# Rows of the experts gathered by a table of tokens, in place of rows scattered to their slots

## The chip, the cores and the metric

The kernel runs on one core of a Trainium2 chip. That core has TensorE (PE), VectorE (DVE), ScalarE (ACT), GpSimd (POOL) and SyncE (SP), and 16 DMA engines that all queues share. The metric is the time of one execution on the device, in microseconds, the median of several runs.

## What is computed

One step of a two-layer network over 640 tokens (128 context, 512 latent) of 1024 numbers. Layer 0 mixes tokens by attention, layer 1 by retention; each is followed by a mixture of 16 experts in 4 groups. The part that matters here, shortened:

```python
scores = sigmoid(x @ router_w)
grouped = (scores + router_b).reshape(n, 4, 4)
group_score = sum(top_k(grouped, 2)[0], axis=-1)       # the two best of each group
best = argmax(group_score)                             # one group per token
_, idx = top_k(where(group == best, grouped, -inf), 2) # two experts of that group
wts = take(scores, idx) / sum
# blocks of 128 slots, each of one expert; every (token, expert) pair gets a slot
xb = x[tok]                                            # rows of a block
hid = silu(xb @ w_gate[e]) * (xb @ w_up[e])
yb = (hid @ w_down[e]) * wt
y = zeros_like(x).at[row_tok].add(yb)
```

640 tokens with 2 experts each make 1280 pairs. Slots that hold no pair may compute anything, since nothing reads their result with a weight.

## The kernel before, in words

The program is a sequence of stages. Each stage is a block in which every engine has its own list of instructions, ordered by semaphores; all engines pass the end of a stage together. The stages are: setup, modulation, the attention's projection (`mla_project`) and its head pairs, then routing, experts and combine of layer 0, then retention, routing, experts and combine of layer 1, and the output.

**Routing** (`route`, L1430 to L1627). SP issues six weight loads of 2 MB for the first two expert blocks. The normed activations lie with features on the partitions. PE makes the router's logits, then turns all activations into token rows (L1585), which ScalarE copies to the tile `rows` (L1613). VectorE runs one long chain in which each instruction waits for the one before (`link`): the scores, the sum of the two best of each group as the maximum over the six pair sums (L1498 to L1502), the best group, the two best experts as one-hots, the weights, and after PE's prefix sums the row number of both slots of each token (`dest`, L1549). Each expert owns one block of 128 slots, and pairs past 128 go to further blocks, whose expert is worked out at the tail of the chain (L1552 to L1562), together with the number of block pairs to run. POOL waits for `dest` and writes the rows to the DRAM tensor `rows_in` by ten indirect DMAs (L1625): five token tiles, two slots each. It waits for all ten.

**Experts** (`experts`, L1641 to L1952). A loop over blocks of 128 slots, two per turn, as many turns as the routing found (18 blocks in each layer here). Per block POOL loads 128 consecutive rows of `rows_in` (L1695), PE turns them (L1746), ScalarE and VectorE split rows and weights into a high and a low part (L1826, L1895), and PE makes three products for each (L1758). SP refills a weight slot when its last part has been split (L1638). ScalarE stores each result block to `rows_out` (L1851). A refill of rows waits until PE has turned the block two before it (L1699).

**Combine** (`combine`, L1955). POOL gathers both result rows of each token with ten indirect DMAs (L1968) by `dest`.

Because slots without a token are read too, `mla_project` writes zeros over all of `rows_in` (26 stores, L491) and over ten blocks of `rows_out` (L493), from SP.

## Time and profile before

| | us |
|---|---|
| median of 3 runs | 2322.36 (2321.2 to 2327.05) |
| the profiled execution | 2347.12 |
| its span, first to last instruction | 2345.4 |
| PE busy | 2061.8 (88%) |
| VectorE busy | 1155.7 (49%) |
| ScalarE busy | 894.8 (38%) |
| POOL busy | 119.6 (5%) |

The span is what the rows below are timed in. Busy time counts an engine's instructions only, not its waits; the times of PE are modelled at their ends. An entry of a timeline gives start, duration, engine, line, output and inputs, count, and in brackets how long the engine had been idle and what released it.

### The profile page before, as it was taken

What the parts mean: (1) busy time and instruction counts of PE and PEld (TensorE: products, weight loads), DVE (VectorE), ACT (ScalarE), POOL (GpSimd) and SP (SyncE); (2) the same over time, 40 slices, a digit from 0 to 9 for tenths busy, and PEclk for the clock granted to TensorE, in tenths of its full rate; (3) what the DMA queues carried; (4) which work ended last, traced back from release to release, by engine and by line L of the source; (5) the groups of instructions that cost most, each with busy time, mean ns of one, the idle gap of its engine ahead of it and who ended that gap; (6) DMA issues with size and microseconds to landing.
All of it is one profiled execution on the core that took longest, in us unless ns stands there. A gap on an engine that the chain in (4) does not pass through costs nothing. (4 is left out here: it accounts for less than half of the span.)

```text
span 2345.4 us, 25093 instructions
## 1 busy us (share of the span) xinstructions
PE 2061.8 (88%) x8790; PEld 1428.8 (61%) x8790; DVE 1155.7 (49%) x1688; ACT 894.8 (38%) x1251; POOL 119.6 (5%) x139
## 2 busy tenths in 40 slices
PE   4878999999749999958999999999999948999984
PEld 2334545544438878837756865875676427878863
DVE  1122223222559999955322422322242347999975
ACT  1011212212238888824211221221122127888853
POOL 0000000000020000011000100100010010000001
PEclk8679889887869999968999999999999968999995
DMA  9995000100569999734211220221110078999933
GB/s 356 387 379 215 19 28 9 37 18 0 215 234 385 399 399 399 296 139 155 81 45 55 72 90 18 72 81 63 45 63 18 2 303 295 399 399 398 398 151 135
DMA packets 181343, 425.26 MB, mean 181 GB/s; under 512 B 10622, under 2 KB 22427, under 8 KB 181275
## 3 DMA queue, kind: packets, MB, share of 16 engines
q1 hardware_dynamic: 164912, 365.52, 42.3%
q0 software_dynamic: 10944, 39.85, 4.5%
q10 hardware_dynamic: 5418, 18.96, 2.0%
q8 instruction: 45, 0.74, 0.1%
q14 instruction: 24, 0.19, 0.0%
HBM read 369.09 MB, written 55.21 MB: 181 GB/s over the span
## 5 line engine op out<-in xcount | busy, mean ns | idle before, releaser
L1895 DVE TENSOR_TENSOR moe_w_lo<-weight_ring,moe_w_hi 128x1024 fp32r<-128x1024 f32 x432 | 520.3, 1222 | 84.4 <-ACT moe_w_hi L1826 70.2
L1826 ACT ACTIVATE moe_w_hi<-weight_ring 128x1024 fp32r<-128x1024 f32 x432 | 456.5, 1061 | 192.7 <-PE ps L1758 124.5
L1758 PE MATMUL ps<-moe_w_hi,moe_rows_t_hi 128*128 128x512 f32 x576 | 232.8, 404 | 5.1 <-DVE moe_rows_t_lo L1900 4.7
L1305 DVE TENSOR_TENSOR ret_w_lo<-weight_ring,ret_w_hi 128x512 fp32r<-128x512 f32 x128 | 95.4, 746 | 274.5 <-ACT ret_w_hi L1227 274.5
L1758 PE MATMUL ps<-moe_w_hi,moe_rows_t_lo 128*128 128x512 f32 x576 | 226.5, 393 | 0.0
L1758 PE MATMUL ps<-moe_w_lo,moe_rows_t_hi 128*128 128x512 f32 x576 | 226.0, 392 | 0.0
L1100 PE MATMUL ps<-ret_w_hi,h_hi 128*128 128x512 f32 x480 | 193.9, 404 | 3.6 <-ACT weight_ring L1231 2.5
L1227 ACT ACTIVATE ret_w_hi<-weight_ring 128x512 fp32r<-128x512 f32 x128 | 80.8, 635 | 302.8 <-PE ps L1100 299.9
L1100 PE MATMUL ps<-ret_w_lo,h_hi 128*128 128x512 f32 x480 | 189.6, 395 | 0.0
L1100 PE MATMUL ps<-ret_w_hi,h_lo 128*128 128x512 f32 x480 | 189.5, 395 | 0.0
L1758 PEld LDWEIGHTS ps<-moe_w_hi,moe_rows_t_hi 128*128 128x128 f32 x576 | 109.5, 190 | 27.1 <-DVE moe_rows_t_lo L1900 5.5
L1758 PEld LDWEIGHTS ps<-moe_w_hi,moe_rows_t_lo 128*128 128x128 f32 x576 | 109.1, 189 | 23.7
L1758 PEld LDWEIGHTS ps<-moe_w_lo,moe_rows_t_hi 128*128 128x128 f32 x576 | 109.6, 190 | 20.8
L1758 PE MATMUL ps<-moe_w_hi,moe_hidden_t_hi 128*128 128x512 f32 x288 | 114.6, 398 | 3.0 <-DVE moe_hidden_t_lo L1905 3.0
L1758 PE MATMUL ps<-moe_w_lo,moe_hidden_t_hi 128*128 128x512 f32 x288 | 113.8, 395 | 0.0
L1758 PE MATMUL ps<-moe_w_hi,moe_hidden_t_lo 128*128 128x512 f32 x288 | 113.7, 395 | 0.0
L1212 PE MATMUL ps<-weight_ring 128*128 128x512 f32 x256 | 110.9, 594 | 2.9 <-ACT weight_ring L1292 2.9
L1100 PEld LDWEIGHTS ps<-ret_w_hi,h_hi 128*128 128x128 f32 x480 | 90.0, 187 | 29.3 <-issue 5.3
L1100 PEld LDWEIGHTS ps<-ret_w_lo,h_hi 128*128 128x128 f32 x480 | 90.0, 188 | 23.0 <-issue 1.9
L1100 PEld LDWEIGHTS ps<-ret_w_hi,h_lo 128*128 128x128 f32 x480 | 90.0, 187 | 22.0
L1187 PE MATMUL ps<-weight_ring 128*128 128x512 f32 x224 | 99.7, 593 | 2.2 <-DVE weight_ring L1316 2.2
L307 PE MATMUL ps<-weight_ring,silu_cond 128*32 128x512 f32 x384 | 67.5, 841 | 33.4 <-DMA weight_ring<-in_ada_w 20.6
(303 smaller groups left out, 2979.9 us busy)
## 6 DMA issues: line engine op xcount, KB each, us to landing
weight_ring<-in_moe_w_gate SPq DMA_DIRECT2D x36, 2048.0 KB, 13.7
weight_ring<-in_moe_w_up SPq DMA_DIRECT2D x36, 2048.0 KB, 14.7
weight_ring<-in_moe_w_down SPq DMA_DIRECT2D x36, 2048.0 KB, 14.1
weight_ring<-in_ada_w SPq DMA_DIRECT2D x24, 2048.0 KB, 19.8
weight_ring<-in_ret_w_in SPq DMA_DIRECT2D x12, 2048.0 KB, 9.1
h_normed<-rows_in POOLq DMA_DIRECT2D x36, 512.0 KB, 7.1
rows_out<-h_normed ACTq DMA_DIRECT2D x36, 512.0 KB, 6.3
rows_in<-zero_rows SPq DMA_DIRECT2D x26, 512.0 KB, 15.1
```

Source lines behind the costliest of these rows:

```text
L307: mm = pe.matmul(ps[32 * j:32 * j + 32, n % 4, :], cond[:, k, :], weights(n)[:, k, :], start=(half == 0), stop=(half == 1), tile_position= ...
L1100: mm = pe.matmul(out, lhs, rhs, start=(k == 0 and x == 0), stop=(k == KD - 1 and x == 2))
L1187: mm = pe.matmul(out, lhs, rhs, start=(x == 0), stop=(x == len(mms) - 1))
L1212: mm = pe.matmul(ps[:, bank(f"w{d}"), :], wo[:, b, d * P:(d + 1) * P], yt[:, b, SEQ:T], start=(b == 0), stop=(b == 3))
L1227: nc.scalar.activation(whi[:, n % BUF, :], win[s][:, k, :], ACT.Identity).then_inc(w_hi, 1)
L1305: dve.tensor_tensor(wlo[:, n % BUF, :], win[s][:, k, :], whi[:, n % BUF, :].bitcast(F32), ALU.subtract).then_inc(w_lo, 1)
L1758: mm = pe.matmul(out, lhs, rhs, start=(first and x == 0), stop=(last and x == 2))
L1826: nc.scalar.activation(whi[:, x, :], part(u, w + x), ACT.Identity).then_inc(w_hi, 1)
L1895: dve.tensor_tensor(wlo[:, x, :], part(blk[1], w + x), whi[:, x, :].bitcast(F32), ALU.subtract).then_inc(w_lo, 1)
```

## The change

In routing ScalarE stores the token rows plainly to the first 640 rows of `rows_in` (five stores). VectorE makes, beside `dest`, for each slot index k and token tile a one-hot of the slot's place in its block (128 wide) and a one-hot of its block (26 wide) multiplied by the token's number. PE multiplies the two and sums over tokens, which gives a table of 128 places by 26 blocks that holds the token of each slot, and 0 where a slot has none. VectorE copies it to `tok` as integers. POOL's scatters are gone. In the expert loop POOL copies the block's column of the table and gathers the 128 rows by it. The 26 stores of zeros to `rows_in` are gone; those to `rows_out` stay. The sum of a group's two best is made from maxima and minima of pairs: 7 instructions in place of 11. Two constants (a row 0 to 127 and the token numbers) come by a small load at the start of routing. Semaphores of the combine live through both layers, and five small tiles of retention become parts of one.

```diff
-            one * np.arange(NBLK), p % 32 == np.arange(NE)]
+            one * np.arange(NBLK), p % 32 == np.arange(NE), one * np.arange(P), p + P * np.arange(NT)]
...
-        self.xs = ops["rows_in"]
+        self.xs = ops["rows_in"][0:T, :]
...
-                for b in range(NBLK):
-                    sp.dma_start(c.xs[b * P:(b + 1) * P, :], zeros[:, :]).then_inc(zeros_out, 16)
...
+                sp.dma_start(consts[:, :], c.ops["base_consts"][:, _width(BASE_COLS):]).then_inc(const_in, 16)
                 prefetch(sp)
...
+                link(dve.tensor_scalar(by_row[:, :], c.base["iotab"], float(P), None, ALU.mult))
...
-                m = gr[:, :, :].rearrange("p t (g e) -> p (t g) e", e=EG)
-                link(dve.tensor_tensor(pair[:, 0, :], m[:, :, 0], m[:, :, 1], ALU.add))
-                for a in range(EG):
-                    for b in range(max(a + 1, 2), EG):
-                        link(dve.tensor_tensor(pair[:, 1, :], m[:, :, a], m[:, :, b], ALU.add))
-                        link(dve.tensor_tensor(pair[:, 0, :], pair[:, 0, :], pair[:, 1, :], ALU.max))
-                first_best(keep[:, :, :], pair[:, 0, :].rearrange("p (t g) -> p t g", t=NT), NG)
+                grouped = gr[:, :, :].rearrange("p t (g e) -> p (t g) e", e=EG)
+                two = gr[:, :, :].rearrange("p t (h e) -> p (t h) e", e=2)
+                more, less = top2[:, 0, :], top2[:, 1, :]
+                link(dve.tensor_tensor(more, two[:, :, 0], two[:, :, 1], ALU.max))
+                link(dve.tensor_tensor(less, two[:, :, 0], two[:, :, 1], ALU.min))
+                more, less = (x.rearrange("p (g h) -> p g h", h=2) for x in (more, less))
+                first, second, third = top2[:, 2, 0:G], top2[:, 2, G:2 * G], top2[:, 3, 0:G]
+                link(dve.tensor_tensor(first, more[:, :, 0], more[:, :, 1], ALU.max))
+                link(dve.tensor_tensor(second, more[:, :, 0], more[:, :, 1], ALU.min))
+                link(dve.tensor_tensor(third, less[:, :, 0], less[:, :, 1], ALU.max))
+                link(dve.tensor_tensor(second, second, third, ALU.max))
+                link(dve.tensor_tensor(first, first, second, ALU.add))
+                first_best(keep[:, :, :], first.rearrange("p (t g) -> p t g", t=NT), NG)
...
-                mark["dest"] = n
+                link(dve.tensor_scalar(slot_i[:, :, :], c.dest[:, :, :], P - 1, None, ALU.bitwise_and))
+                link(dve.tensor_copy(slot[:, :, :], slot_i[:, :, :]))
+                link(dve.tensor_tensor(blk[:, :, :], dst[:, :, :], slot[:, :, :], ALU.subtract))
+                dve.wait_ge(const_in, 16)
+                for k in range(2):
+                    link(dve.tensor_tensor(at_slot[:, k], m["iota"].unsqueeze(1).to_broadcast([P, NT, P]),
+                                           slot[:, k, :].unsqueeze(2).to_broadcast([P, NT, P]), ALU.is_equal))
+                    for t in range(NT):
+                        link(dve.tensor_scalar(at_blk[:, k, t, :], by_row[:, :], blk[:, k, t:t + 1], m["token"][:, t:t + 1],
+                                               ALU.is_equal, ALU.mult))
+                    mark[f"at{k}"] = n
...
+                dve.wait_ge(mapped, 1)
+                dve.tensor_copy(c.tok[:, :], ps[:, 7, 0:NBLK])
...
+                    pe.wait_ge(chain, mark[f"at{k}"])
+                    for t in range(NT):
+                        mm = pe.matmul(ps[:, 7, 0:NBLK], at_slot[:, k, t, :], at_blk[:, k, t, :],
+                                       start=(k == 0 and t == 0), stop=(k == 1 and t == NT - 1))
+                mm.then_inc(mapped, 1)
...
+                    if g % 2:
+                        act.wait_ge(taken, g + 1)
+                        act.dma_start(c.xs[(g // 2) * P:(g // 2 + 1) * P, :], rows[:, g // 2, :]).then_inc(stored, 16)
+                act.wait_ge(stored, 16 * NT)
...
-                pool.wait_ge(chain, mark["dest"])
-                for t in range(NT):
-                    pool.wait_ge(taken, 2 * t + 2)
-                    for k in range(TOPK):
-                        pool.indirect_dma_start(c.xs, bass.IndirectOffsetOnAxis(c.dest[:, k, t:t + 1], 0),
-                                                rows[:, t, :], None).then_inc(scattered, 16)
-                pool.wait_ge(scattered, 16 * NT * TOPK)
...
                 def load_rows(blk):
-                    b, u, _ = blk
-                    pool.dma_start(xr[:, u, :], c.xs.rearrange("(b p) d -> b p d", p=P)[bass.ds(b, 1)].rearrange("a p d -> (a p) d"))\
-                        .then_inc(xfull[u], 16)
+
+                    b, u, i = blk
+                    pool.tensor_copy(tok[:, u:u + 1], c.tok[:, bass.ds(b, 1)]).then_inc(indexed, 1)
+                    pool.wait_ge(indexed, b + 1)
+                    pool.sem_inc(c.asked, 1)
+                    pool.indirect_dma_start(xr[:, u, :], None, c.xs, bass.IndirectOffsetOnAxis(tok[:, u:u + 1], 0)).then_inc(xfull[u], 16)
 
                 def refill_rows(blk):
                     pool.wait_ge(turned, blk[0] - 1)
+                    pool.sem_inc(c.asked, 1)
                     load_rows(blk)
```

## Rows read from the trace of the kernel before

**Rows 1.** The page, part 1: busy us (share of the span) and instructions.

```profile
PE 2061.8 (88%) x8790; PEld 1428.8 (61%) x8790; DVE 1155.7 (49%) x1688; ACT 894.8 (38%) x1251; POOL 119.6 (5%) x139
```

**Rows 2.** Waits, 670 to 1010 us: who, for whom, total, times, longest.

```profile
ACT moe_w_hi L1826 <- PE ps L1758: 62.1, 171, 4.3
```

**Rows 3.** Windows: length, busy by engine, clock, DMA share, GB/s; loop, combine.

```profile
700.00:940.00 240.00, 236.18 (x1107) 192.60 (x1106) 225.76 (x211) 196.37 (x212) 6.99 (x13) 1.00 1.04 395
...
1026.00:1036.00 10.00, 3.83 (x16) 3.13 (x16) 4.49 (x10) 3.44 (x3) 7.06 (x7) 0.50 0.97 359
```

**Rows 4.** Timeline, 600 to 720 us: routing of layer 0.

```profile
609.17 1.01 DVE L898 SCALAR_TENSOR_TENSOR x_resid<-ps,modulation,x_resid 128x128 f32<-128x128 f32 x2 [1.15 <-PE ps L799]
...
610.53 0.31 POOL L1617 MEMSET route_router<- 128x256 f32 x1 [449.29 <-POOLq L681]
...
632.80 4.56 PE L1585 MATMUL ps<-base_consts,h_normed 128*128 128x128 f32 x40
...
633.33 0.20 DVE L1493 TENSOR_SCALAR route_scores<-route_scores 128x80 f32<-128x80 f32 x1 [1.70 <-ACT route_scores L1609]
...
634.53 0.20 DVE L1498 TENSOR_TENSOR route_pair<-route_biased 128x20 f32<-128x20 f32 x1
...
636.78 0.18 DVE L1502 TENSOR_TENSOR route_pair<-route_pair 128x20 f32<-128x20 f32 x1
...
644.29 2.29 PE L1597 MATMUL ps<-route_both,base_consts 128*128 128x16 f32 x10
...
652.18 0.17 DVE L1549 CAST route_rows<-route_dst 128x10 int32<-128x10 f32 x1
...
654.28 0.53 DVE L1562 TENSOR_SCALAR block_pairs<-route_turns 128x1 int32<-128x1 f32 x3
...
664.22 0.95 POOL L1625 DMA_INDIRECT rows_in<-route_rows  x1 [0.31 <-issue]
670.00 1.15 POOL L1695 DMA_DIRECT2D h_normed<-rows_in  x2 [4.82 <-POOLq L1453]
...
671.74 4.63 DVE L1895 TENSOR_TENSOR moe_w_lo<-weight_ring,moe_w_hi 128x1024 fp32r<-128x1024 f32 x4 [16.93 <-ACT moe_w_hi L1826]
...
673.68 1.97 PE L1746 MATMUL ps<-base_consts,h_normed 128*128 128x128 f32 x8 [27.09 <-DMA h_normed<-rows_in]
```

**Rows 5.** Timeline, 1870 to 2000 us: routing of layer 1.

```profile
1917.81 0.17 DVE L1549 CAST route_rows<-route_dst 128x10 int32<-128x10 f32 x1
...
1939.12 1.97 PE L1746 MATMUL ps<-base_consts,h_normed 128*128 128x128 f32 x8 [26.90 <-DMA h_normed<-rows_in]
```

**Rows 6.** Single lines of VectorE: duration in ns, least, median, most.

```profile
L424 DVE TENSOR_TENSOR h_normed<-x_resid,norm_rstd x32: 818/820/826, 164.4 to 2332.5; 128x640 f32<-128x640 f32 x32
...
L430 DVE TENSOR_SCALAR h_normed<-h_normed,norm_amplitude,modulation x16: 341/344/348, 165.8 to 1893.8; 128x128 f32<-128x128 f32 x16
```

**Rows 7.** DMA issues, KB, median us to landing: 700 to 940, then 900 to 960.

```profile
rows_out<-h_normed ACTq DMA_DIRECT2D x13, 512.0 KB, 6.3
...
weight_ring<-in_moe_w_gate SPq DMA_DIRECT2D x3, 2048.0 KB, 15.2
```

**Rows 8.** Lines 1695 (loads of rows) and 1968 (combine's gathers): issues, landing.

```profile
L1695 POOL DMA_DIRECT2D h_normed<-rows_in x36: 527/537/584, 670.0 to 2209.4; - x36
...
DMA to landing us min/median/max: 3.5/7.1/7.8
...
DMA to landing us min/median/max: 4.3/5.6/6.2
```

**Rows 9.** Timeline of SP and POOL in the expert loop of layer 0.

```profile
677.12 0.38 SPq L1638 DMA_DIRECT2D weight_ring<-in_moe_w_gate  x1
...
743.12 0.54 POOL L1695 DMA_DIRECT2D h_normed<-rows_in  x1 [17.73 <-PE ps L1746]
```

**Rows 10.** Zero stores in the attention's projection (timeline), and a wait of SP.

```profile
154.09 27.10 SPq L491 DMA_DIRECT2D rows_in<-zero_rows  x26
...
SPq L495 <- DVE mla_new_cache L599: 38.2, 1, 38.2
```

More of the change, by code:

```diff
@@ L73 @@
 BASE_COLS = {"ident": P, "ones": P, "before": P, "iota16": NE, "iota4": NG, "iotab": NBLK, "pick": NE}
+ROUTE_COLS = {"iota": P, "token": NT}
 MLA_COLS = {"swap": P, "rcos": LAT, "rsin": LAT}
@@ L148, in __init__ @@
         self.w_in_full, self.wq_full, self.wkv_full, self.wo_full = sems(nc, stack, "mla", ["w_in", "wq_full", "wkv_full", "wo_full"])
+        self.comb_sems = sems(nc, stack, "comb", ["weighed", "summed", "turned", "added"])
+        self.got = sems(nc, stack, "comb", [f"got{t}" for t in range(NT)])
+        self.asked, = sems(nc, stack, "moe", ["rows_asked"])
         self.ret_full = sems(nc, stack, "ret", [f"full{s}" for s in range(4)])
-        self.xs = ops["rows_in"]
+        self.xs = ops["rows_in"][0:T, :]
         self.ys = ops["rows_out"]
@@ L1022, in retention @@
         qd = sb("q_decayed", [P, 2, LAT])
-        kd, lg = sb("k_decay", [P, 2]), sb("log_decay", [P, 2])
-        sumsq, mean, rs = sb("sumsq", [P, NT, 2]), sb("meansq", [P, NT, 2]), sb("rstd", [P, NT, 2])
+        small = sb("small", [P, 4 + 6 * NT])
+        kd, lg = small[:, 0:2], small[:, 2:4]
+        sumsq, mean, rs = (small[:, 4 + 2 * NT * x:4 + 2 * NT * (x + 1)].rearrange("p (t f) -> p t f", f=2) for x in range(3))
         half = c.half[:, 0:2]
@@ L1442, in route @@
                                              ("scores", "biased", "masked", "one1", "one2", "both", "tmp", "past"))
-        pair, keep, off = sb("pair", [P, 2, G]), sb("keep", [P, NT, NG]), sb("off", [P, NT, NG])
+        consts = sb("consts", [P, _width(ROUTE_COLS)])
+        m = _views(consts, ROUTE_COLS)
+        slot_i = sb("slot_int", [P, 2, NT], I32)
+        slot, blk = sb("slot", [P, 2, NT]), sb("block", [P, 2, NT])
+        at_slot, at_blk = sb("at_slot", [P, 2, NT, P]), sb("at_block", [P, 2, NT, NBLK])
+        top2, keep, off = sb("pair", [P, 4, 2 * G]), sb("keep", [P, NT, NG]), sb("off", [P, NT, NG])
         top = sb("top", [P, NT])
@@ L1448, in route @@
         cmp, eb, tn = sb("compare", [P, NBLK - NE, NE]), sb("block_e", [P, NBLK]), sb("turns", [P, 2])
+        by_row = sb("block_rows", [P, NBLK])
         logits_t = sb("logits_t", [P, T])
         norm = Norm(c, st, 2 * layer + 1, amp, shift)
-        padded, by_expert, copied_a, copied_v, logits, ranks, turned, taken, expd, chain, scattered = sems(
-            nc, st, f"route{layer}", ["padded", "by_expert", "copied_a", "copied_v", "logits", "ranks", "turned", "taken", "exp", "chain", "scattered"])
+        padded, by_expert, copied_a, copied_v, logits, ranks, turned, taken, expd, chain, const_in, stored, mapped = sems(
+            nc, st, f"route{layer}", ["padded", "by_expert", "copied_a", "copied_v", "logits", "ranks", "turned", "taken", "exp", "chain", "consts", "stored", "mapped"])
         with nc.Block(no_gpsimd_drain=True) as block:
@@ L1598, in _ @@
                 mm.then_inc(ranks, 1)
+                for k in range(2):
+                    pe.wait_ge(chain, mark[f"at{k}"])
[3 more added lines that the diff above has]
+                mm.then_inc(mapped, 1)
             @block.scalar
@@ L1662, in experts @@
         sil, hid = sb("silu", [P, FE]), sb("hidden", [P, FE])
+        tok = sb("tokens", [P, 2], I32)
+        indexed, = sems(nc, st, f"moe{layer}", ["indexed"])
         xfull = sems(nc, st, f"moe{layer}", ["x_full0", "x_full1"])
@@ L1960, in combine @@
         y = st.enter_context(nc.sbuf_tensor(f"comb{layer}_rows", [P, NT, TOPK, D], F32))
-        got = sems(nc, st, f"comb{layer}", [f"got{t}" for t in range(NT)])
-        weighed, summed, turned, added = sems(nc, st, f"comb{layer}", ["weighed", "summed", "turned", "added"])
+        got = c.got
+        weighed, summed, turned, added = c.comb_sems
+        before = layer * NT
         with nc.Block(no_gpsimd_drain=True) as block:
@@ L1979, in _ @@
                 for t in range(NT):
-                    pe.wait_ge(summed, t + 1)
+                    pe.wait_ge(summed, before + t + 1)
                     if t >= 4:
-                        pe.wait_ge(added, (t - 3) * KD)
+                        pe.wait_ge(added, (before + t - 3) * KD)
                     for k in range(KD):
@@ L1991, in _ @@
                     if t < NT:
-                        dve.wait_ge(weighed, t + 1)
+                        dve.wait_ge(weighed, before + t + 1)
                         dve.scalar_tensor_tensor(out=y[:, t, 0, :], in0=y[:, t, 1, :], scalar=c.w12[:, 1, t:t + 1],
@@ L1996, in _ @@
                         n = t - 1
-                        dve.wait_ge(turned, n + 1)
+                        dve.wait_ge(turned, before + n + 1)
                         jc = 0 if n == 0 else 1
```

9 lines of the change are left out of this document (5 added, 4 removed).

## The prediction, made before the result was known

> **What bounds the kernel now.** I read the page first, then the waits of an expert stage, then the stretches of it by window, then the routing stage instruction by instruction. On the page [rows 1] TensorE is busy 88% of the span. Two expert stages (from about 670 us and from about 1936 us) take 36 block turns [rows 8]. The waits of the first [rows 2] say which is late there: ScalarE's weight splits wait for PE 171 times (62.1 us in all), and no weight split waits for a DMA. The loop's stretch [rows 3] shows PE busy 236.18 of 240 us at full clock, and DMA share 1.04 at 395 GB/s: PE sets the pace, DMA is just short of setting it. So the expert loop is expensive, but what the change shortens lies before it, where PE is idle 27.1 us [rows 4].
>
> In the first layer's routing [rows 4] VectorE runs one dependent chain of small instructions, one start every 0.21 to 0.28 us, and finishes the slot numbers at 652.35. POOL then issues ten scatters, 1.26 us apart, 652.67 to 665.17. It waits for them to land, all engines pass the stage's end, and POOL issues the first load of rows at 669.97. The rows land and PE starts to turn them at 673.68. From the end of the slot numbers to the first turned row: 673.68 - 652.35 = 21.33 us. In the second layer [rows 5] it is 1939.12 - 1917.98 = 21.14 us. Nothing else is late in that time: the first four weight splits end at 676.4 on VectorE [rows 4], and the turned rows, which take 2 us on PE and then both engines in turn, come after them.
>
> **The change part by part, per layer.**
>
> Two best of a group. Before, 11 instructions, 634.53 to 636.99, 2.46 us [rows 4]. After, 7: two over 40 elements (between the 0.18 us of 20 and the 0.24 of 80; I take 0.21), three over 20 strided at 0.20, two over 20 plain at 0.18, each with 0.03 to the next: 0.48 + 0.69 + 0.42 = 1.6 us. Saved 0.86 us. The added product for the block rows stands ahead of a wait in which VectorE idles 1.70 us: free.
>
> Longer chain on VectorE after the slot numbers:
> - three instructions on 10 elements at about 0.17 + 0.03 each: 0.62 us;
> - two comparisons of 128x640. The row is the norm's product of that size, 0.82 us [rows 6]; with the gap 0.85, so 1.70 us;
> - ten instructions on 26 elements with two scalars read from SBUF. No row is that form: at 128 elements it takes 0.344 us [rows 6], a plain one on 20 elements 0.18 us [rows 4]. Taking off 102 elements at the 0.24 - 0.18 us per 60 of the chain's rows gives 0.24; with the gap 0.26, so 2.6 us. Ends: 2.1 to 3.7 us.
> Then the old tail, from 652.35 to 654.81 (its last three start at 654.28), 2.46 us [rows 4]. PE's last five products of 26 columns start beside that tail. Their nearest row is the count of the experts, ten records in 2.29 us [rows 4]: with the handover, hidden to within 0.1 us. The copy of the table adds 0.2. From slot numbers to VectorE's end: 0.62 + 1.70 + 2.6 + 2.5 + 0.2 = 7.62 us (7.1 to 9.0).
>
> Ten scatters removed. With them go their 12.5 us of issue, the landing of the last, and 10 x 512 KB of writes. What is late next is VectorE's end above.
>
> Five stores from ScalarE. They are issued from about 634.5 to 641, while the six weight loads still run. Those are 12.6 MB from 611 us and end near 643 at the loop's 395 GB/s [rows 3]. Adding 2.6 MB puts everything down by about 650. In the expert loop, where DMA is as full, a 512 KB store lands in 6.3 us [rows 7]. VectorE ends at 652.35 - 0.86 + 7.62 = 659.1, so 9 us of cover. The weights pushed back by 6.7 us are first needed after 659. Were the cover gone, each us past it would cost one. The ScalarE issues stretch the copies by some 2 us and PE's turning by as much; PE's turning now ends at 637.4 and PE is next wanted some 4.8 us later, five instructions before its count at 644.29 [rows 4], so that is covered too. SP issues one 68 KB load ahead of its six: 0.4 us, hidden for the same reason.
>
> Start of the experts. The last stage change of this kind took 0.35 us from VectorE's last instruction (610.18) to POOL's first (610.53) [rows 4]. POOL then copies one column (no row; its fill of 256 elements takes 0.31 us [rows 4], so I take 0.25 with the wait, ends 0.1 and 0.6) and issues a gather in place of a plain load. The plain load landed 3.5 us after its issue at best, the combine's gathers 4.3 at best, 5.6 in the median when ten queue up [rows 8]. The first stands alone, so 4.3, with ends 3.5 and 6.2.
>
> Sum, from slot numbers to the first turned row: -0.86 + 7.62 + 0.35 + 0.25 + 4.3 = 11.66 us. Saved: 21.33 - 11.66 = 9.67 and 21.14 - 11.66 = 9.48; together **19.2 us**. Ends: 11 to 22 us. The loop starts that much earlier whichever engine bounds it, since DMA too stands still before its first refill at 677.12 [rows 9].
>
> The Trainium skill gives a different price for that first gather: "DMA: Bandwidth & Descriptors", section on the anatomy of a SWDGE DMA, fits 2.0 us plus the bytes at 436 GB/s, which is an estimate of 3.2 us for 512 KB. The rows show 3.5 for the plain load and 4.3 for a gather, so the trace disagrees and I keep 4.3; by the skill's fit the sum would be 21.4 us.
>
> Gathers inside the loop. POOL refills a row buffer as soon as it is turned, and idles 17.7 us between refills [rows 9]; a dearer issue (0.95 of a scatter [rows 4] against 0.54 us), a copy and a wait vanish in that. Bytes and packets are the same 512 KB.
>
> Zero rows. The 26 stores of zeros are issued 154.1 to 181.2, ten more behind them; SP then waits 38.2 us for VectorE's last row of the stage [rows 10]. Nothing of value is freed: 0 us. Renamed semaphores, the constants' split and the shared small tile change no instruction on the path: 0.
>
> The profiled execution took 2347.12 us (span 2345.4), the median of the timed ones 2322.36, 1.1% less. 2347.12 - 19.2 = 2327.9; for the median 2322.36 - 19.2 x 0.989 = **2303.4 us**.
>
> **Rivals.**
>
> A, slower: the row that all empty slots read. 18 blocks have 2304 slots, 1280 hold a token, and the other 1024 now read token 0, 57 slots a block, 0.233 MB from one 4 KB row. Before, each slot had its own row. DMA has no room: three 2 MB loads, a load of rows and a store are 7.34 MB, and a block turn takes 17.73 + 0.54 = 18.27 us [rows 9]: 402 GB/s. A weight slot is used every second block, 36.5 us; its four parts are split in a third of a turn, 6 us, so about 30 us are left from refill to next use, and the load takes 15.2 us late in the stage [rows 7], some with 2 us more: 13 us of slack. If those 57 reads cost e more per block, the loop loses 18e - 13 us per layer. It decides from e = 0.72 us, and eats the gain at e = (13 + 9.6)/18 = 1.26 us, which is the row served at 0.233 MB/(0.58 + 1.26 us) = 127 GB/s. At a quarter of full rate (100 GB/s, e = 1.75) each layer loses 18.5 and gains 9.6: +17.8 us, 2340 us. For it: nothing in this trace reads one row many times, and DMA is full. Against it: the combine's gathers of scattered rows run at 359 GB/s [rows 3], no worse than plain traffic.
> The Trainium skill has a rule of this sort ("DMA: Bandwidth & Descriptors", section on latency and other measured facts): streams in step on aliased HBM rows fell from 207 to 103 GB/s. No run here shows it; halved, e is 0.6 us and hides in the slack.
>
> B, smaller gain: the chain and the first gather come out at their dear ends (9.0, 6.2, copy 0.6, some wait for PE), 5.5 to 6 us saved per layer: 2311 us. For it: several forms have no row, and the first gather already reads the shared row. Against it: the chain's other rows are very regular.
>
> C, no change: the scatters were not what held the stage, because the stores of ScalarE land late, queued behind 12.6 MB of weights. They would have to land at 669, 18 us after the sum of bytes allows. Gain 0, 2322 us. Against it: the 6.3 us landing in the full loop.
>
> **How the numbers follow.** Forecast 0.74, A 0.07 (slower) and 0.02 (its loss near the gain, no change), B 0.14, C 0.03. The likeliest own range is 2299 to 2309. The 8 in 10 range takes B in: 2298 to 2311. A measurement here tells about 0.3% (7 us) from no change: faster 0.74 + 0.14 = 0.88, same 0.02 + 0.03 = 0.05, slower 0.07.
>
> **What would show it.** Ten instructions of the 26-element form per layer at about 0.24 us; VectorE's part of the routing ending 6.8 us after where its slot numbers ended; POOL starting the experts some 10.5 us earlier against the routing's start; a first gather landing in about 4.3 us; the block period still 18.2 to 18.3 us with no weight split waiting for a DMA. Wrong it would be if that period grows, if weight loads take over 25 us, or if the routing stage ends on ScalarE's stores.

## The result

On the chips on which both kernels ran, the kernel before had a median of 2332.4 us over 22 runs (2316.0 to 2352.1) and the changed one 2319.0 us over 22 (2301.5 to 2334.1). The ratio is 0.9939, 95% interval [0.9915, 0.9964]: 14.2 us less (8.4 to 19.8). Run again, the changed kernel gave 2320.6 us over 12 runs against 2331.5 over 14: 0.9957 [0.992, 0.9994]. Three more runs of the kernel before, at 2350.8 to 2352.8 us, fell into a slower state of the chip and are left out there. The forecast was 2303.4 us, from 2298 to 2311. So it named the right side and missed the size: the gain is smaller than the 19.0 us forecast, and the kernel before, too, is 10 us slower over 22 runs than over the three that were known.

The profiled execution of the changed kernel took 2334.08 us (span 2331.9, granted clock 0.915), 13.0 us less than that of the kernel before. Its page, part 1 (busy time, share and instructions by engine), answers to [rows 1]:

```profile
span 2331.9 us, 25267 instructions
...
PE 2070.7 (89%) x8830; PEld 1438.1 (62%) x8830; DVE 1164.7 (50%) x1714; ACT 895.8 (38%) x1251; POOL 141.3 (6%) x155
```

POOL is busy 22 us longer, for its gathers are dearer to issue than plain loads. It waits for most of each turn, so this costs nothing in the loop. The loop itself, as in [rows 3] (length, busy time by engine, clock, DMA share, GB/s):

```profile
691.00:931.00 240.00, 236.17 (x1106) 192.54 (x1106) 225.71 (x211) 196.41 (x212) 24.41 (x26) 1.00 1.04 395
```

PE is busy 236.17 of 240 us, before 236.18, at the same DMA share. Thirteen blocks, from the start of turning block 2 to that of block 15, took 237.05 us, before 236.99.

The routing of layer 0 in the changed kernel, as in [rows 4] (start, duration, engine, line, operation, count, idle time before it and what ended it):

```profile
609.42 0.31 POOL L1660 MEMSET route_router<- 128x256 f32 x1 [449.11 <-POOLq L684]
...
633.43 0.20 DVE L1515 TENSOR_TENSOR route_pair<-route_biased 128x40 f32<-128x40 f32 x1
...
634.75 0.18 DVE L1523 TENSOR_TENSOR route_pair<-route_pair 128x20 f32<-128x20 f32 x1
634.97 0.17 DVE L1497 TENSOR_REDUCE route_top<-route_pair 128x5 f32<-128x20 f32 x1
...
639.72 0.33 ACTq L1655 DMA_DIRECT2D rows_in<-route_rows  x1
...
650.06 0.17 DVE L1570 CAST route_rows<-route_dst 128x10 int32<-128x10 f32 x1
650.27 0.17 DVE L1571 TENSOR_SCALAR route_slot_int<-route_rows 128x10 int32<-128x10 int32 x1
...
650.89 0.82 DVE L1576 TENSOR_TENSOR route_at_slot<-route_consts,route_slot 128x640 f32<-128x640 f32 x1
651.75 1.64 DVE L1579 TENSOR_SCALAR route_at_block<-route_block_rows,route_block,route_consts 128x26 f32<-128x26 f32 x5
...
654.29 1.64 DVE L1579 TENSOR_SCALAR route_at_block<-route_block_rows,route_block,route_consts 128x26 f32<-128x26 f32 x5
655.96 0.33 DVE L1583 TENSOR_TENSOR route_compare<-route_cumulated,base_consts 128x160 f32<-128x160 f32 x1
655.98 2.33 PE L1635 MATMUL ps<-route_at_block,route_at_slot 128*128 128x26 f32 x10 [0.20 <-DVE route_at_block L1579]
...
658.42 0.18 DVE L1595 CAST block_tokens<-ps 128x26 int32<-128x26 f32 x1 [0.17 <-PE ps L1635]
658.96 0.18 POOL L1734 COPY moe_tokens<-block_tokens 128x1 int32<-128x1 int32 x1 [41.67 <-POOLq L1466]
660.04 1.17 POOL L1737 DMA_INDIRECT h_normed<-rows_in,moe_tokens  x1 [0.90 <-POOL moe_tokens L1734]
...
664.47 1.97 PE L1788 MATMUL ps<-base_consts,h_normed 128*128 128x128 f32 x8 [6.16 <-DMA h_normed<-rows_in,moe_tokens]
```

The reader sees the whole path of the change here: slot numbers done at 650.23, VectorE done at 658.60, first gather issued at 660.04, PE starts to turn the first rows at 664.47. That is 8.37 + 1.44 + 4.43 = 14.24 us, where it was 21.33. In layer 1 it is 13.92, where it was 21.14. From start to slot numbers the stage took 40.81 and 41.57 us, before 41.82 and 43.12.

The table gives these parts for every kernel profiled, in us (the experiments that the names stand for follow below): from routing's start to the slot numbers; from there to VectorE's end, to the gather's issue and to the first turned row, with their sum; then from the issue of the last store of the experts to the first gather of the combine. A dash stands where a kernel has no such part.

```
kernel, layer     start-slots  VectorE  to issue  to row    sum   store-combine
before       0       41.82        -        -       3.68    21.33      3.85
before       1       43.12        -        -       3.61    21.14      3.81
changed      0       40.81       8.37     1.44     4.43    14.24      5.97
changed      1       41.57       8.36     1.35     4.21    13.92      3.75
again        0       40.77       8.36     1.44     4.44    14.24      5.98
again        1       39.67       8.35     1.35     4.27    13.97      3.76
two_best     0       41.53        -        -       3.72    21.36      3.84
two_best     1       41.73        -        -       3.65    21.20      3.81
zeros_kept   0       41.50       8.35     1.43     4.48    14.26      5.97
zeros_kept   1       41.42       8.35     1.35     4.24    13.94      3.74
pad24        0       39.63       8.35     1.44     4.51    14.30      3.76
pad24        1       41.56       8.37     1.35     4.26    13.98      3.74
pad64        0       39.64       8.37     1.44     4.43    14.24      3.77
pad64        1       41.59       8.37     1.69     4.23    14.28      3.75
no_copy      0       41.49       8.36     1.09     4.56    14.01      3.78
no_copy      1       41.75       8.37     0.99     4.23    13.59      3.77
wide_blocks  0       39.63       7.08     1.44     4.65    13.17      6.13
wide_blocks  1       39.92       7.08     1.35     4.24    12.67      3.76
own_rows     0       41.52       8.42     1.43     4.06    13.92      6.49
own_rows     1       41.66       8.42     1.34     3.99    13.76      3.74
one_row      0       41.52       8.36     1.43     4.55    14.34      6.18
one_row      1       41.52       8.36     1.34     4.47    14.17      3.75
warm         0       41.47       8.36     1.44     5.42    15.22      5.97
warm         1       41.49       8.36     1.35     5.31    15.02      3.75
best         0       41.53       7.08     1.10     4.65    12.83      3.77
best         1       41.74       7.08     0.99     5.68    13.75      3.76
best2        0       40.76       6.00     1.09     4.64    11.73      3.77
best2        1       41.74       6.00     0.99     4.81    11.80      3.76
```

Between the two executions of the changed kernel the sum repeats to 0.1 us. The last column is where the unforeseen part stands.

### The profile page after: what moved, and what is told of

The parts are those of the page before. It is cut to its first block and busy times, and to the rows that moved or that the text cites. A ratio compares the mean times of both kernels' runs of the same rounds, so it can differ in the third digit from the quotient of the medians.

```text
span 2331.9 us, 25267 instructions
## 1 busy us (share of the span) xinstructions
PE 2070.7 (89%) x8830; PEld 1438.1 (62%) x8830; DVE 1164.7 (50%) x1714; ACT 895.8 (38%) x1251; POOL 141.3 (6%) x155
## 6 DMA issues: line engine op xcount, KB each, us to landing
weight_ring<-in_moe_w_gate SPq DMA_DIRECT2D x36, 2048.0 KB, 13.9
weight_ring<-in_ada_w SPq DMA_DIRECT2D x24, 2048.0 KB, 19.8
```

## The experiments

**again.** No edit.

> The changed kernel unaltered, once more. Theory M (the path saved 8.1 and 8.8 us instead of 9.7 and 9.5, all else that differs between the two traces is how one execution differs from the next): routing start to first turned row 55.0 to 55.6 us in both layers again, retention within 1 us of the 818.1 us of the kernel before or anywhere 816 to 822, with no fixed +2.5; the ratio to the kernel before about 1 - 16.9/2340 = 0.9928. Rival S (the change also slows a stage outside its own, retention by 2.5 us and the passage into the first combine by 2.1 us): both extra times are there again, and the ratio is 0.994 or above.

Measured: the part from slot numbers to the first row was 14.24 and 13.97 us, as in the first execution to 0.05 us. Retention (from POOL's norm to the start of routing) took 820.48 us, in the kernel before 818.10, and the passage into the first combine 5.98 us again. So the second of rival S's two extra times is real and repeats. The first can't be put down to the change: the kernel before with nothing but the shorter two-best sum (below) has 821.67 us there, the other eleven profiles 820.43 to 823.84, and why that one execution of the kernel before is the shortest is open. The interval of the ratio 0.9957 holds both 0.9928 and 0.994, so the total doesn't decide between the theories.

**two_best.** The kernel before, with its eleven instructions of the two-best sum (L1498 to L1502) exchanged for the seven of the changed kernel.

```diff
...
-                        link(dve.tensor_tensor(pair[:, 1, :], m[:, :, a], m[:, :, b], ALU.add))
-                        link(dve.tensor_tensor(pair[:, 0, :], pair[:, 0, :], pair[:, 1, :], ALU.max))
...
+                link(dve.tensor_tensor(more, two[:, :, 0], two[:, :, 1], ALU.max))
+                link(dve.tensor_tensor(less, two[:, :, 0], two[:, :, 1], ALU.min))
...
```

> The kernel before with only the shorter sum of the two best. Both theories: the two-best part takes 1.54 us instead of 2.46, routing start to first turned row 62.2 and 63.4 us instead of 63.15 and 64.26; gain 1.8 us in all, less than one execution differs from the next. If the wait behind it were on something else (the count products on TensorE), the part would be shorter and the routing not.

Measured: 604.72 to 606.26, 1.54 us against 2.46. From slot numbers to the first row 21.36 and 21.20 us, as in the kernel before: the two halves of the change are independent. From the start of routing to the first turned row it took 62.89 and 62.93 us, so layer 0 shows 0.3 of the 0.9 us and layer 1 1.3: with the same instructions the first half of the stage varies by 2 us between executions (table, first column, kernels with the shorter sum: 39.6 to 41.8), so the totals can't show the 0.9 us.

**zeros_kept.** The changed kernel with the zero stores put back.

```diff
+                for b in range(NBLK):
+                    sp.dma_start(c.ops["rows_in"][b * P:(b + 1) * P, :], zeros[:, :]).then_inc(zeros_out, 16)
```

> The changed kernel, but the 26 stores of zero rows are issued as before. Theory M (they cost nothing): attention 457.4 to 457.8 us either way, routing unchanged at 55.0 and 55.5 us. Rival: they cost 0.4 us or more in attention (SP issues 27 us longer beside it), then attention comes back at 457.8 or above and the sum over the stages behind it is unchanged.

Measured: attention 434.63 us and the sum 14.26. The attention time can't be set against 457.4, for this stage varies by 30 us with the granted clock (see below): own_rows, which has no zero stores, shows 434.58 us in an execution with the same granted clock there (0.92), pad24 435.29. At equal clock the stores cost nothing that shows beside that 0.7 us. The forecast's zero holds.

**own_rows, one_row.** Where the table is copied from PSUM, every slot of it is overwritten: with token rows 0 to 127 in one kernel, with row 0 in the other. Both compute other rows than the reference asks for.

```diff
-                dve.tensor_copy(c.tok[:, :], ps[:, 7, 0:NBLK])
+                dve.tensor_scalar(c.tok[:, :], ps[:, 7, 0:NBLK], 0.0, m["token"][:, 0:1], ALU.mult, ALU.add)   # own_rows
+                dve.tensor_scalar(c.tok[:, :], ps[:, 7, 0:NBLK], 0.0, None, ALU.mult)                          # one_row
```

> The changed kernel, where each block gathers token rows 0 to 127 whatever its slots hold (the experts therefore work on other rows than the reference's; traffic and instructions are the same). No row is read more than once by a block. Theory M (a row read many times costs nothing here): first gather lands 4.2 to 4.4 us after its issue, gathers in the loop 7.0 to 8.9 us, block turn 18.23 us, all as in the changed kernel. Rival H (the shared token row costs): first gather at 3.5 us, gathers in the loop 1 us or more shorter, weight loads shorter than 13.1 us, and, if it had cost time in the full loop, a turn under 18.2 us.

> The changed kernel, where every slot of every block gathers token row 0 (all 128 rows of a gather are one 4 KB row, 36 times; the experts therefore work on other rows than the reference's). Theory M (a shared row costs nothing): first gather to first turned row 4.4 us, gathers in the loop 7 to 9 us, block turn 18.23 us. Rival H (the row is served at a limited rate): with 128 instead of 57 reads of it per block the cost would be 2.2 times what the changed kernel pays, and would show in the first gather, which stands almost alone: over 4.4 us, and in the loop's turn.

Measured in layer 0 (in layer 1 the routing sees other data and runs two blocks more, so the totals of 2346.3 and 2340.5 us say nothing). The windows of 680 to 880 us and the DMA issues (count, KB, median us to landing) of 680 to 900 us, first of own_rows:

```profile
680.00:880.00 200.00, 196.78 (x924) 160.59 (x923) 188.36 (x177) 163.73 (x176) 19.93 (x22) 1.00 1.04 397
...
weight_ring<-in_moe_w_up SPq DMA_DIRECT2D x12, 2048.0 KB, 14.3
h_normed<-rows_in,moe_tokens POOLq DMA_INDIRECT x12, 7.4
```

then of one_row:

```profile
680.00:880.00 200.00, 196.77 (x924) 160.38 (x923) 188.42 (x176) 163.36 (x177) 19.92 (x22) 1.00 1.04 399
...
weight_ring<-in_moe_w_up SPq DMA_DIRECT2D x12, 2048.0 KB, 15.1
h_normed<-rows_in,moe_tokens POOLq DMA_INDIRECT x12, 7.7
```

PE is busy the same 196.8 us in both, and thirteen blocks take 236.8 and 236.9 us. With the one row read 128 times a block, the gathers land 0.3 us and these weight loads 0.8 us later at the median. The kernels that gather the right rows have 7.3 to 7.7 us for the gathers over as long a part of the loop, so the 0.3 us is not clear of what executions differ by; for the weight loads they have 13.9 to 14.8 us, so the one row's 15.1 lies just above. The slack hides it. At the first gather, which stands on the path, there is a trace of rival A: in layer 0 4.06 us with own rows, 4.43 to 4.51 in the changed kernel and its padded forms, 4.55 with the one row; in layer 1 3.99, 4.21 to 4.27 and 4.47. So the full row read 128 times costs 0.5 us at the first gather, and the changed kernel pays 0.4 and 0.2 to 0.3 us over own rows. Own rows also lie one behind the other, and the changed kernel's do not, so how much of its part is the shared row is not shown. In the loop it costs nothing.

**pad24, pad64.** 24 or 64 semaphore increments that nobody waits for, on POOL in the routing of layer 0, behind its last work there. They change nothing but the length of POOL's program.

```diff
                 norm.pool_root(pool)
+                if layer == 0:
+                    for _ in range(24):
+                        pool.sem_inc(c.asked, 1)
```

> The changed kernel with 24 idle semaphore increments on POOL in the first routing, after its last work there, where POOL waits some 40 us anyway. In four runs of the changed kernel and its variants the first combine's first gather starts 5.97 to 6.49 us after ScalarE issues the last store, against 3.84 us in two of the old loop; in the same microseconds an 8 KB packet of an instruction queue moves. Theory F (POOL's instructions are fetched in blocks and the longer loop moved a block's border to where the stage ends): with other borders the first combine starts 3.8 us after that store, and 2.1 us come back there or turn up at another place of POOL's program. Rival theory (the ends of the gathers' own queue or semaphores cost it): 5.97 us stays. Routing start to first turned row 55.0 to 55.8 us either way.

> As the run with 24, with 64 increments. Theory F: another border again; the wait before the first combine is 3.8 or 6 us by where it falls, and need not be as with 24. Rival theory: 5.97 us with both.

Measured: the end of the experts and the start of the combine, first in the changed kernel (timeline of ScalarE's and POOL's queues; then the DMA queues of the last 2 us before that gather):

```profile
1009.41 0.34 ACTq L1893 DMA_DIRECT2D rows_out<-h_normed  x1
...
1015.38 0.94 POOL L2011 DMA_INDIRECT comb_rows<-rows_out,route_rows  x1 [78.62 <-issue]
...
q14 instruction: 1, 0.01, 1.0%
```

and with 24 increments:

```profile
986.63 0.34 ACTq L1896 DMA_DIRECT2D rows_out<-h_normed  x1
...
990.39 0.94 POOL L2014 DMA_INDIRECT comb_rows<-rows_out,route_rows  x1 [76.58 <-SPq L2009]
```

With 24 increments the wait is 3.76 us, with 64 3.77. The 2.2 us are gone, the packet on the queue called "instruction" too, and POOL's gather is released by the stage's end instead of by "issue". With 24 no other part of the table grew by more than 0.1 us; with 64 the first gather of layer 1 started 0.34 us later (1.69 us after VectorE's end), which no other execution shows and which stays open. Theory F is borne out: adding 24 instructions made the program 2.2 us shorter at this place. In the 4 us before that gather an 8 KB packet of an instruction queue stands in all seven executions that wait 5.97 us or more (in two of them beside one of 16 KB), and in none of the seven that wait 3.76 to 3.85. The chip isn't the cause: pad24, pad64 and wide_blocks ran on one chip, and the last waits 6.13 us.

The Trainium skill describes such a thing ("Runtime: NRT & Kernel Launch", Instruction fetch mechanics): the sequencer fetches its code in blocks, sequentially, and a taken branch out of what it holds waits for a fetch. The traces agree with it in kind: the wait comes where POOL leaves its loop. In the changed kernel POOL's sequencer branches out of the loop at 1012.13, signals the stage's end at 1012.36 and issues the gather only at 1015.38, 3.0 us later, with padding 0.8 us later. Whether the branch or the plain end of a block of code brings the fetch, and that a border lies exactly there, is inferred from the padding, not read.

**no_copy.** The first two gathers, whose blocks are constants, take their column of the table in place.

```diff
-                    pool.tensor_copy(tok[:, u:u + 1], c.tok[:, bass.ds(b, 1)]).then_inc(indexed, 1)
-                    pool.wait_ge(indexed, b + 1)
+                    # static blocks only:
+                    pool.indirect_dma_start(xr[:, u, :], None, c.xs, bass.IndirectOffsetOnAxis(c.tok[:, b:b + 1], 0)).then_inc(xfull[u], 16)
```

> The changed kernel, where the first two gathers of the experts read their column of the table in place, with no copy and no wait ahead of them. Theory M (copy and handover cost 1.0 to 1.1 us each layer): the first gather is issued 0.2 to 0.3 us after POOL starts the stage instead of 1.1; routing start to first turned row 54.1 and 54.6 us, 0.9 less in each layer. Rival theory (the 0.9 us between copy and gather is the gather's own preparation and comes whatever stands before it): 55.0 and 55.5 us as now. Total: 1.8 us less, under what one run differs from the next.

Measured, the start of the experts in layer 0 (VectorE ended at 637.16):

```profile
636.98 0.18 DVE L1595 CAST block_tokens<-ps 128x26 int32<-128x26 f32 x1 [0.17 <-PE ps L1635]
638.25 1.17 POOL L1735 DMA_INDIRECT h_normed<-rows_in,block_tokens  x1 [41.79 <-POOLq L1466]
...
639.73 0.94 POOL L1735 DMA_INDIRECT h_normed<-rows_in,block_tokens  x1 [0.31 <-issue]
```

The gather starts 1.09 us after VectorE's end instead of 1.44 (layer 1: 0.99 instead of 1.35). So the copy with its wait costs 0.35 us, and of the 0.9 us that stand between copy and gather most come with no copy too. My theory was wrong by two thirds, the rival right for that much.

The kernel before narrows down where the rest comes from. Its first scatter of layer 0 and the first gather of its combine:

```profile
652.67 1.20 POOL L1625 DMA_INDIRECT rows_in<-route_rows  x1 [34.28 <-DVE route_rows L1549]
...
1021.82 1.01 POOL L1968 DMA_INDIRECT comb_rows<-rows_out,route_rows  x1 [77.63 <-SPq L1963]
```

The scatter, in the middle of a stage and after an idle time of 34 us, starts 0.3 us after the slot numbers (652.35). The gather, the first work of a stage, starts 0.85 us after POOL's sequencer has signalled the stage's end (1020.97), and the first plain load of the experts 0.63 us after it (669.36, 670.00). In no_copy that time is 0.86 us (637.39, 638.25). So the first indirect DMA of a stage is late, and not every one that follows no other. Why is open.

The shorter program of POOL had no fetch before the combine (3.78 us). The ratio is 0.9877 [0.9801, 0.9952], which is 29 us. The parts explain 17 (14 for the change, 0.6 for the copies, 2.2 for the fetch): the four runs had a mean granted clock of 0.924, the seven of the kernel before beside them 0.916, so this total is no price of the edit.

**wide_blocks.** The ten block comparisons as three wide instructions.

```diff
-                    for t in range(NT):
-                        link(dve.tensor_scalar(at_blk[:, k, t, :], by_row[:, :], blk[:, k, t:t + 1], m["token"][:, t:t + 1],
-                                               ALU.is_equal, ALU.mult))
+                link(dve.tensor_tensor(flat_blk, by_row..., blk..., ALU.is_equal))              # 260 elements, once
+                link(dve.tensor_tensor(at_blk[:, k], at_blk[:, k], m["token"]..., ALU.mult))    # 130 elements, for each k
```

> The changed kernel with the ten 26-element instructions (two scalars from SBUF, 0.33 us each with the gap, 3.34 us) done as three instructions over 130 to 260 elements. Theory M (VectorE's chain is the path, one for one): the three take about 0.35 + 0.28 + 0.28 and gaps, 1.0 us; the chain is 2.3 us shorter and so is routing start to first turned row: 52.7 and 53.2 us. Rival theory (the table's products on TensorE or the stores of ScalarE end the stage almost as late): less than 1.5 us comes back.

Measured:

```profile
627.91 0.43 DVE L1576 TENSOR_TENSOR route_at_block<-route_block_rows,route_block 128x260 f32<-128x260 f32 x1
628.37 0.29 DVE L1578 TENSOR_TENSOR route_at_block<-route_at_block,route_consts 128x130 f32<-128x130 f32 x1
...
629.58 4.46 PE L1638 MATMUL ps<-route_at_block,route_at_slot 128*128 128x26 f32 x20 [8.10 <-DVE route_at_slot L1580]
...
634.15 0.18 DVE L1598 CAST block_tokens<-ps 128x26 int32<-128x26 f32 x1 [1.11 <-PE ps L1638]
```

The three take 1.1 us with their gaps in place of 3.34, but the chain is only 1.29 us shorter (7.08): the last line now waits 1.11 us for TensorE. Its ten products, which run as twenty records in 4.46 us at a granted clock of 0.50 (1.2 GHz), became the path. The rival's limit of 1.5 us holds. Slot numbers to the first row: 13.17 and 12.67 us. The ratio is 0.9895 [0.9811, 0.9979]; these runs, too, had a higher granted clock (0.923) than the kernel before beside them (0.916).

**warm.** Four products of 384 columns on TensorE ahead of the first turned row, their result not used.

```diff
                 last = turns(pe, 1)
+                for _ in range(NWARM):
+                    pe.matmul(ps[:, 7, 0:3 * P], c.base["ones"], c.base_tile[:, 0:3 * P], start=True, stop=True)
```

> The changed kernel with four idle products of 384 columns on TensorE between the end of routing and the first turned row, where it waits 6.2 us. Theory M (the first 10 to 13 products of the gate run at 1.2 GHz because TensorE had been idle; part of what differs between traces is where the clock rises): the granted clock is at 2.4 GHz within 1 us of the gate's start, and first turned row to the first combine takes 3 to 4 us less in each layer (layer 0 about 345 without the 2.1 us stall before the combine, 347 with it; layer 1 about 344). Rival theory (the clock's rise is not set by what TensorE did just before): no difference, 347 to 351 and 347 to 349 us.

Measured in layer 0: the granted clock was 1.00 while the rows were turned and fell back to 0.50 in the gate (the experts' first products) that follows, after TensorE had idled 2.4 us. The idle products also ran past the landing of the rows: 5.42 us to the first row instead of 4.43, in layer 1 5.31 instead of 4.21. From first turned row to the last store it took 342.68 and 342.82 us instead of 344.94 and 343.85. Of the 2.3 and 1.0 us that came back so, the delay took 1.0 and 1.1. Neither theory's numbers hold.

**best, best2.** best is wide_blocks, no_copy and warm together. best2 adds five such idle products ahead of the table's products.

```diff
+                for _ in range(5):
+                    pe.matmul(ps[:, 7, 0:3 * P], c.base["ones"], c.base_tile[:, 0:3 * P], start=True, stop=True)
                 for k in range(2):
                     pe.wait_ge(chain, mark[f"at{k}"])
```

> The changed kernel with three edits: block one-hots in three wide instructions, the first two gathers with no copy, and the four idle products. Theory M: 1.1 us from the chain, 0.3 us from the copy (both measured singly), 3 us from the clock per layer, and 2.1 us of the instruction fetch in layer 0 once: 11 us under the changed kernel, a ratio to the kernel before of 0.989 to 0.990. Rival theory (idle products cost later: the clock is granted less elsewhere): ratio 0.994 to 0.996 as the changed kernel.

> The kernel 'best' with five more idle products of 384 columns on TensorE in the routing, ahead of the table's products. Theory M (the ten plus ten table products take 4.5 us because they run at 1.2 GHz, and they end the stage once VectorE's chain is short): they take 2.3 us, VectorE no longer waits for them, and 0.9 to 1.0 us more comes back in each layer: 13 us under the changed kernel. Rival theory (the clock has not risen by then, and the idle products only delay the table's): the same as 'best' or up to 2 us slower.

Measured: best 0.9886 [0.9834, 0.9938], best2 0.9876 [0.9824, 0.9929] (2311.4 and 2311.0 us, six runs each, against 2338.3 over 11). In best2 VectorE no longer waits for the table (6.00 us), and the sum is 11.73 and 11.80. The start of the experts in windows of 3, 2 and 5 us from the first turned row, first no_copy:

```profile
642.81:645.81 3.00, 1.96 (x8) 1.56 (x8) 1.58 (x2) 1.00 (x1) 0.18 (x1) 0.50 0.29 116
645.81:647.81 2.00, 0.67 (x2) 0.57 (x3) 1.22 (x1) 0.02 (x1) 0.96 (x1) 0.50 0.64 158
647.81:652.81 5.00, 5.00 (x17) 3.98 (x16) 1.23 (x1) 1.91 (x2) 0.00 (x0) 0.70 1.01 369
```

then best2:

```profile
653.01:656.01 3.00, 1.04 (x9) 0.80 (x7) 2.37 (x3) 1.02 (x1) 1.00 (x2) 1.00 0.27 105
656.01:658.01 2.00, 1.59 (x7) 1.33 (x8) 0.35 (x1) 0.00 (x0) 0.29 (x1) 1.00 0.64 178
658.01:663.01 5.00, 5.00 (x28) 4.24 (x27) 3.47 (x3) 3.94 (x4) 0.00 (x0) 1.00 1.02 385
```

Twenty-eight products in the 5 us instead of seventeen, at a granted clock of 1.00 throughout. In layer 1 of best2 it is the same; best, with only the four products ahead of the rows, has 1.00 throughout in layer 0 too, but 0.92, 0.73 and 0.77 in layer 1. First turned row to the last store: 341.26 and 341.36 us, against 343.4 to 345.3 in the kernels that gather and have no idle products. By the parts, best2 saves (14.24 - 11.73) + (13.92 - 11.80) + 2.2 for the fetch and 3.7 + 2.5 for the products ahead of the store: 13.0 us on the changed kernel. The last two are rough, for without idle products that stretch varies by 1.9 us by itself. Its interval lies wholly below 0.993, that of the changed kernel above 0.9915, so its lead over the changed kernel is likely and not shown by the totals alone; nor is one of the two shown faster than the other.

## Why the prediction was right or wrong

The path and the sign were right. What failed is, in this order of size: the time the sum was taken from (10.0 us), a wait in the next stage that the forecast put at nothing (2.1 us), and two terms of the sum that were too small, the start of the experts (0.8 us per layer) and the ten 26-element instructions (0.7 us per layer).

**The view of the bound** was right. The loop did not move, no weight split waits for a DMA, and what went is the time between the slot numbers and the first turned row.

**Two best:** forecast 0.86 us saved, measured 0.92.

**Three 10-element instructions and two comparisons:** 0.62 and 1.70 forecast, 0.66 and 1.73 measured.

**Ten 26-element instructions:** 2.6 forecast, 3.34 measured, 0.33 each with the gap. This is the first mis-sized term, 0.7 us per layer. The row I scaled down, 0.344 us at 128 elements [rows 6], has the very form, two scalars read from SBUF. I took off 102 elements at 0.001 us each, the slope of the plain form (0.18 to 0.24 us for 20 to 80), and that slope did not hold: 26 elements take 0.30 us, so the 102 elements are worth 0.04 us and the rest belongs to the form. The forecast had 3.7 as its dear end.

**Tail and table copy:** 2.5 and 0.2 forecast, 2.64 measured from 655.96 to 658.60, the 0.17 us of waiting for TensorE among it. Together VectorE took 8.37, forecast 7.62.

**Start of the experts to the gather:** 0.35 + 0.25 forecast, 1.44 and 1.35 measured. This is the second mis-sized term, 0.8 us per layer and beyond its dear end (0.95). The copy itself cost about what I said, as no_copy shows (0.35). What I left out is the start of a stage's first indirect DMA: 0.7 us even with no copy ahead. I took the 0.35 us of a stage whose first instruction on POOL is a fill. The trace of the kernel before had the nearer row, the first gather of its combine, 0.85 us after the stage's end.

**Landing:** 4.3 forecast, 4.43 and 4.21 measured. The own rows' 4.06 and 3.99 are nearer 4.3 too than the 3.2 us that the fit of the Trainium skill ("DMA: Bandwidth & Descriptors", anatomy of a SWDGE DMA) gives as an estimate for 512 KB.

So from slot numbers to the first row 12.52 us were forecast (11.66 with the two-best's saving) and 14.24 and 13.92 measured. Per layer 7.1 and 7.2 us plus 0.92 were saved: 16.1 us in all, where 19.2 were forecast.

**The stage after**: 2.1 us were lost before the first combine, where the forecast had nothing. This is the step of the gain that fails as a mechanism, not as a size. The prediction asked what the gathers in the loop cost in time, and found POOL idle. It did not ask what a longer program costs, where POOL leaves the loop. 16.1 - 2.1 = 14.0 us, and the measured ratio is 14.2 us. That they meet so closely is luck, for the ratio's interval is 8.4 to 19.8 us, which holds the forecast's 19.0 us too; what shows the parts are the traces.

**Scatters, stores, zeros:** right. ScalarE's last store was issued at 639.72; the slowest of the ten took 11.0 us to land, so by 650.7, 8 us ahead of VectorE's end.

**Rival A** is refuted for the loop and true to at most 0.5 us a layer at the first gather. **Rival B** is right in direction only: it has 5.5 to 6 us saved per layer, the forecast 9.6, and 8.0 and 8.1 were measured. The chain came out between forecast and dear end (8.37 us), the landing at its forecast, only the passage to the gather beyond its dear end; the fetch stands in no rival. **Rival C** is refuted.

**The absolute time** failed at one more step, the last of the forecast and the largest miss of all: "2322.36 - 19.2 x 0.989". The three known runs (2321.2 to 2327.1) were taken for the kernel's time. Over 22 runs it is 2332.4 with 36 us from least to most. Of the 15.6 us by which 2319.0 misses 2303.4, 10.0 stand here and 5.6 in the gain. The profile already said so: it took 2347.12 us, 25 more than the median beside it, and I divided it away.

The traces show where such a difference comes from, though none is of the kernel before at 2322 us. The attention stage, from about 152 to 610 us, has the same instructions in all kernels, but took 457.8, 457.4 and 457.7 us in three executions, 427.95 in two and 434.6 to 448.1 in the others. The window of that stage (150 to 580 us), in the changed kernel and in two_best:

```profile
150.00:580.00 430.00, 397.21 (x1308) 213.80 (x1309) 131.58 (x307) 102.03 (x208) 2.13 (x2) 0.87 0.10 36
```

```profile
150.00:580.00 430.00, 394.17 (x1392) 215.00 (x1392) 142.08 (x329) 103.16 (x210) 2.63 (x4) 0.94 0.18 67
```

About the same busy time of PE, but 1308 products done in it or 1392: granted clock 0.87 or 0.94. The span of two_best is 31.1 us shorter than that of the kernel before, and 29.8 of them stand in this stage. In order of that clock the stage takes 457.4 us (0.87), 448.1 (0.89), 441.0 (0.91), 434.6 to 435.5 (0.92) and 427.95 (0.94). Over all 35 runs of the kernel before whose clock is known the time falls with the mean granted clock at a correlation of -0.98. In the changed kernel TensorE was granted 0.50 from 452.5 to 483.2 us and was busy for 93% of it; in the 147 us ahead it had been granted 1.00 and was busy for 95%. Such stretches, behind the stage's first 90 us, add up to 95 us in the changed kernel and to 27 in two_best; half of the 68 us between them, at 93% busy, is an estimate of 32 us against 29.5 measured. What decides in an execution how long they are is open.

## What to carry to other kernels

Price an instruction from the row of its own form, even if its size is far off, and don't scale it by the slope of another form: with two scalars from SBUF it took 0.30 us at 26 elements and 0.344 at 128. Price the first DMA of a stage from the first DMA of another stage. Count an engine's program as well as its busy time, since a change of its length can move an instruction fetch onto the path; if the first instruction after a loop waits for "issue", padding or unpadding that engine is a cheap test. When the profiled execution and the few timed runs differ by more than the gain expected, forecast the ratio and widen the time by that difference.

## What the runs showed of the hardware

- When an indirect DMA on POOL starts depends on what stands before it: 0.30 us behind another one, 0.3 us after the slot numbers in the middle of a stage (kernel before), 0.79 to 0.90 us behind a copy on POOL and a semaphore increment, and 0.80 to 0.86 us after POOL has signalled a stage's end, where no fetch stands between.
- POOL's code fetch: 2.2 us after its loop (up to 2.7 in own_rows), with an 8 KB packet of an instruction queue, gone with 24 instructions more.
- A gather that reads one 4 KB row 128 times lands 0.5 us later than one of 128 different rows that lie one behind the other (4.55 against 4.06 us, in layer 1 4.47 against 3.99). In the full loop PE's pace is the same.
- The granted clock of the experts' first products changed with what TensorE did before: nine idle products before and between brought it to 1.00 from the first turned row on in both layers, four alone in one of the four stages that had them (best, layer 0), in the others it fell to 0.60 to 0.73.
- In the attention stage, with TensorE 92% busy and the same instructions, the mean granted clock varies from 0.87 to 0.94 between executions, and the stage by 30 us.
